# Differential attention: two maps in three adjacent PSUM banks, scores two units ahead, the maps added on GpSimd

## The reference

```
def diff_attention(q, k, v, lam):            # q, k: 4 heads x 2 maps x 64; v: 4 heads x 128
    ...
    def block(qi):                           # blocks of 128 queries
        s = jnp.einsum("bhqtd,bhktd->tbhqk", qi, k).astype(jnp.float32) * scale
        pr = jax.nn.softmax(s, axis=-1)
        a = pr[0] - lam * pr[1]
        return jnp.einsum("bhqk,bhkv->bhqv", a.astype(v.dtype), v)
    ...
o_da = (rmsnorm(o_da, p["da_subln"]) * (1.0 - lam_init))
```

## Time and profile before

| what | value |
|---|---|
| median of three runs | 2616.13 us (2613.88 to 2620.17) |
| time of the profiled execution | 2614.22 us |
| its span, first to last instruction | 2612.5 us |
| PE busy, share of the span | 2406.2 us, 92% |
| DVE busy | 949.7 us, 36% |
| ACT busy | 629.8 us, 24% |
| POOL busy | 403.7 us, 15% |

### The profile page before, as it was taken

One profiled execution on the slowest core, in us unless ns is written; L12 is line 12 of the kernel. 1 busy time (PEld: TensorE's weight loads), 2 busy tenths in 40 slices (PEclk: granted clock), 3 DMA queues, 4 the chain that ended last, 5 costly groups with the idle time before them and its releaser, 6 DMA issues. The chain is left out here.

```text
span 2612.5 us, 36229 instructions
## 1 busy us (share of the span) xinstructions
PE 2406.2 (92%) x13804; PEld 1439.5 (55%) x13804; DVE 949.7 (36%) x1850; ACT 629.8 (24%) x1519; POOL 403.7 (15%) x456
## 2 busy tenths in 40 slices
PE   5999999989999999899779999998999999989995
PEld 2445644466557655555445565545655765555552
DVE  1423411473106423522364143137410642452226
ACT  2223401350015003122132252016001510312221
POOL 0003100021002300133410030000300230013333
PEclk7999999999999999899879999999999999999998
DMA  8443146100544030589653221220022403155985
GB/s 318 160 162 122 65 149 224 43 1 33 169 145 115 33 125 23 200 332 405 241 218 125 86 94 40 84 73 1 33 89 81 129 33 110 39 204 207 377 343 215
DMA packets 170173, 368.55 MB, mean 141 GB/s; under 512 B 38564, under 2 KB 52140, under 8 KB 170036
## 3 DMA queue, kind: packets, MB, share of 16 engines
q1 hardware_dynamic: 121876, 261.49, 27.4%
q10 hardware_dynamic: 24480, 54.76, 6.0%
q0 software_dynamic: 23680, 50.43, 5.9%
HBM read 344.19 MB, written 47.56 MB: 150 GB/s over the span
## 5 line engine op out<-in xcount | busy, mean ns | idle before, releaser
L228 PE MATMUL ps<-hT,ring 128*128 128x512 f32 x512 | 230.9, 605 | 6.3 <-PEq L1147 2.7
L2513 PE MATMUL ps<-ring,mixT 128*32 128x256 f32 x2688 | 214.0, 382 | 2.9 <-DMA ring<-in_w_e_up 2.5
L237 PE MATMUL ps<-ring,hT 128*128 128x512 f32 x480 | 211.9, 598 | 5.1 <-PEq L1191 4.1
L2513 PEld LDWEIGHTS ps<-ring,mixT 128*32 128x32 f32 x2688 | 120.3, 111 | 95.7 <-issue 21.8
L228 PEld LDWEIGHTS ps<-hT,ring 128*128 128x128 f32 x512 | 96.7, 193 | 130.4 <-issue 130.2
L237 PEld LDWEIGHTS ps<-ring,hT 128*128 128x128 f32 x480 | 90.5, 192 | 115.5 <-issue 113.6
L1278 PE MATMUL ps<-late,ring 128*128 128x320 f32 x512 | 147.2, 447 | 7.6 <-PEq L1366 3.9
L2391 PE MATMUL ps<-ring,mixT 128*128 128x512 f32 x320 | 142.1, 603 | 9.2 <-DVE out_xn L2680 4.8
L1278 PEld LDWEIGHTS ps<-late,ring 128*128 128x128 f32 x512 | 99.6, 196 | 52.9 <-issue 14.8
L1229 POOL TENSOR_TENSOR mix_S<-ring 128x512 f32<-128x512 f32 x16 | 25.2, 1577 | 651.1 <-POOLq L1366 550.1
L664 PE MATMUL ps<-hT,ring 128*128 128x512 f32 x256 | 114.5, 601 | 2.9 <-ACT ssm_dec L916 2.9
(11 more groups left out here) (475 smaller groups left out, 4164.1 us busy)
## 6 DMA issues: line engine op xcount, KB each, us to landing
ring<-in_w_in SPq DMA_DIRECT2D x18, 2048.0 KB, 9.8
ring<-in_w_gate SPq DMA_DIRECT2D x12, 2048.0 KB, 10.1
ring<-in_w_e_down SPq DMA_DIRECT2D x48, 512.0 KB, 17.2
ring<-in_w_e_gate SPq DMA_DIRECT2D x40, 512.0 KB, 5.3
ring<-in_w_e_up SPq DMA_DIRECT2D x40, 512.0 KB, 6.6
co_yg<-y_rows SPq DMA_DIRECT2D x40, 512.0 KB, 5.3
mixT<-in_w_ada ACTq DMA_DIRECT2D x8, 2048.0 KB, 8.7
da_ada_w<-in_w_ada ACTq DMA_DIRECT2D x8, 2048.0 KB, 8.8
```

The lines of the kernel that those rows point to most:

```text
L228: pe.matmul(lat, wide[:, k, c], hT[:, k, CTX:TOK], start=(k == 0), stop=(k == kt_n - 1))
L237: last = pe.matmul(out, cx.hT[:, k, tok(t)], wide[:, k, :], start=(k == 0), stop=(k == KT - 1))
L2513: ins = pe.matmul(ps[rows, 2 + b, 0:2 * P].rearrange("p (g f) -> p g f", g=2), xT[:, b, k, rows], ew[:, :, k, :], start=(k == 0), stop=(k ...
```

## The change

It has four parts.

1. **Banks.** The two maps of a unit fill three adjacent banks instead of four: map 0 takes columns 0 to 639 of the three banks' 1536, map 1 the last 640, so that each has one full bank and 128 columns of the middle one. Banks 0 to 2 and 3 to 5 serve in turn. The four products become 512, 128, 512 and 128 columns. The two pieces in the middle bank are kept apart by a new wait of PE, `da_short`, before the last product; and `maxima(u, 1)` waits until the first exponential of its unit has been read, as both touch the middle bank. Maxima and exponentials now read 640 columns in a row.
2. **Two units ahead.** `scores(u+2)` stands where `scores(u+1)` stood, and waits for the second exponential of unit u. `e` gets a third unit (`e_all`, [P, 3, 2, 640]), laid over the rotary tables and lambda, which are done with by then; `sm` gets a third column. ACT's order becomes `exps(u+2, 0)`, `evacuate(u)`, `exps(u+2, 1)`, and DVE's `combine(u)`, `maxima(u+1, 1)`, `maxima(u+2, 0)`, `take(u-1)`.
3. **The maps added on GpSimd.** L1737 goes. DVE ends `combine` with the coefficient; GpSimd then multiplies `e1` by it (128x640) and adds it to `e0` (128x640), and raises `da_a_ready`.
4. `combine(u)` waits also for GpSimd to be done with unit u-2.

```
+            for u in range(len(units)):
+                pool.wait_ge(sem("da_co"), u + 1)
+                e0, e1 = e_all[:, u % 3, 0, :], e_all[:, u % 3, 1, :]
+                pool.tensor_scalar(e1, e1, co[:, u % 2:u % 2 + 1], None, ALU.mult).then_inc(sem("da_scaled"), 1)
+                pool.wait_ge(sem("da_scaled"), u + 1)
+                pool.tensor_tensor(e0, e0, e1, ALU.add).then_inc(sem("da_a_ready"), 1)
...
             def scores(u):
...
-                if u:
-                    pe.wait_ge(sem("da_exp"), 2 * u - 1)
+                if u >= 2:
+                    pe.wait_ge(sem("da_exp"), 2 * u - 2)
...
-                for m in range(2):
-                    pe.matmul(ps[:, b[m], 0:320], q[m], k[m][:, CTX:CTX + 320], start=True, stop=True)
-                for m in range(2):
-                    pe.matmul(ps[:, b[m] + 1, 0:320], q[m], k[m][:, CTX + 320:CTX + 640], start=True,
-                              stop=True).then_inc(sem("da_scores"), 1)
+                short, long = slice(0, KEYS - SEC), slice(KEYS - SEC, KEYS)
+                pe.matmul(to[0][:, 0:SEC], q[0], k[0][:, 0:SEC], start=True, stop=True)
+                pe.matmul(to[1][:, short], q[1], k[1][:, short], start=True, stop=True).then_inc(sem("da_short"), 1)
+                pe.matmul(to[1][:, long], q[1], k[1][:, long], start=True, stop=True).then_inc(sem("da_scores1"), 1)
+                pe.wait_ge(sem("da_short"), u + 1)
+                pe.matmul(to[0][:, SEC:KEYS], q[0], k[0][:, SEC:KEYS], start=True, stop=True).then_inc(
+                    sem("da_scores0"), 1)
...
             def maxima(u, m):
                 n = 2 * u + m
-                dve.wait_ge(sem("da_scores"), n + 1)
-                b = s_banks(n)
-                if n >= 4:
+                dve.wait_ge(sem(f"da_scores{m}"), u + 1)
+                if m:
+                    dve.wait_ge(sem("da_exp"), n)
+                elif n >= 4:
                     dve.wait_ge(sem("da_exp"), n - 3)
...
             def combine(u):
...
                 if u >= 2:
                     dve.wait_ge(sem("da_o_out"), u - 1)
-                step(dve, dve.reciprocal(rc[:, u % 2, :], sm[:, u % 2, :]))
...
-                dve.scalar_tensor_tensor(out=e0, in0=e1, scalar=co[:, u % 2:u % 2 + 1], in1=e0, op0=ALU.mult,
-                                         op1=ALU.add).then_inc(sem("da_a_ready"), 1)
+                    dve.wait_ge(sem("da_a_ready"), u - 1)
+                step(dve, dve.reciprocal(rc[:, u % 2, :], sm[:, u % 3, :]))
+                dve.tensor_scalar(co[:, u % 2:u % 2 + 1], sm[:, u % 3, 0:1], rc[:, u % 2, 1:2], ls[:, 5:6],
+                                  ALU.mult, ALU.mult).then_inc(sem("da_co"), 1)
```

More of the change, by code:

```diff
@@ L1382, in stage_da @@
         nmx = sb("da_nmx", [P, 2, 2])
-        sm = sb("da_sm", [P, 2, 2])
+        sm = sb("da_sm", [P, 3, 2])
         rc = sb("da_rc", [P, 2, 2])
@@ L1425, in _, with score_map @@
             cx.clear_passed(pool)
-        def s_banks(n):
-            return 2 * (n % 3)
+            for u in range(len(units)):
[4 more added lines that the diff above has]
+                pool.tensor_tensor(e0, e0, e1, ALU.add).then_inc(sem("da_a_ready"), 1)
+        KEYS = PAST + LAT
+        def score_map(u, m):
+            unit = ps[:, 3 * (u % 2):3 * (u % 2) + 3, :].rearrange("p b n -> p (b n)")
+            return unit[:, 0:KEYS] if m == 0 else unit[:, 3 * SEC - KEYS:3 * SEC]
         @block.tensor
@@ L1538, in turn @@
                 for c in range(1, 5):
-                    pe.transpose(ps[:, 6, (c - 1) * P:c * P], e[:, u % 2, 0, c * P:(c + 1) * P], cx.ident)
+                    pe.transpose(ps[:, 6, (c - 1) * P:c * P], e_all[:, u % 3, 0, c * P:(c + 1) * P], cx.ident)
                 if u:
                     pe.wait_ge(sem("da_o_out"), u)
-                pe.transpose(ps[:, 7, 0:P], e[:, u % 2, 0, 0:P], cx.ident).then_inc(sem("da_turned"), 1)
+                pe.transpose(ps[:, 7, 0:P], e_all[:, u % 3, 0, 0:P], cx.ident).then_inc(sem("da_turned"), 1)
             def values(u):
@@ L1553, in _ @@
             scores(0)
+            scores(1)
             for u in range(len(units)):
-                if u + 1 < len(units):
-                    scores(u + 1)
+                if u + 2 < len(units):
+                    scores(u + 2)
                 if u:
@@ L1622, in exps @@
                 n = 2 * u + m
-                if u >= 2:
-                    act.wait_ge(sem("da_turned"), u - 1)
+                if u >= 3:
+                    act.wait_ge(sem("da_turned"), u - 2)
+                elif u == 2:
+                    act.wait_ge(sem("da_roped"), 8)
                 else:
@@ L1649, in root @@
                                scale=1.0 / (2 * DA_HD), bias=cx.eps[:, :]).then_inc(sem("da_rms"), 1)
-            exps(0, 0)
-            exps(0, 1)
+            for u in range(2):
+                exps(u, 0)
+                exps(u, 1)
             for u in range(len(units)):
-                if u + 1 < len(units):
-                    exps(u + 1, 0)
-                    exps(u + 1, 1)
-                else:
+                if u + 2 < len(units):
+                    exps(u + 2, 0)
+                elif u + 1 == len(units):
                     root(0, TILES - 1)
                 evacuate(u)
+                if u + 2 < len(units):
+                    exps(u + 2, 1)
                 if u == 2:
@@ L1758, in _ @@
             maxima(0, 1)
+            maxima(1, 0)
             for u in range(len(units)):
@@ L1761, in _ @@
                 if u + 1 < len(units):
-                    maxima(u + 1, 0)
                     maxima(u + 1, 1)
+                if u + 2 < len(units):
+                    maxima(u + 2, 0)
                 if u:
```

26 lines of the change are left out of this document (11 added, 15 removed).

## The result

The changed kernel takes 2632.22 us in the median (2624.69 to 2651.11, 20 runs) against 2617.47 us (2607.46 to 2632.6, 20 runs) for the kernel before on the same chip: ratio 1.0063, 95% interval [1.005, 1.0077]. It is slower by 14.75 us by the medians and by 16 by the ratio (13 to 20 by its interval). Forecast were 2610 us and a range of 2602 to 2621. Its profiled execution took 2629.01 us, with a span of 2627.2. Three executions that lasted 5011 to 7336 us (one each of e4, of e10 and of the kernel before) are in no ratio.

What follows compares the result with a forecast made beforehand. A ring of waits through DVE, 3.92 us per unit, was taken to bound the loop; 66.05 us per layer becoming 63.0 saved 6.1 us in two layers, giving 2610 us, range 2602 to 2621.

Steps and rivals of the forecast that it cites:

- What bounds the loop: Loop before the change: no engine is full, a ring of waits sets the pace at 3.92 us per unit.
- DVE's ring: DVE's cycle before the change: reciprocal, adding the maps, maxima, wait for the second exponential; 3.92 us per unit.
- The new ring: Changed loop: cycle through GpSimd spanning two units, 4.57 us plus scale and add, 7.10 us, 3.55 per unit.
- What GpSimd takes: GpSimd's two steps on 640 columns: scaling 1.0 us (between 0.79 and 1.29), add 1.53 us.
- The bank layout: Score products of 512 and 128 columns: no added cost, at most 0.25 us per unit.
- Rival B: Score products start strictly one behind the other: scores 1.53 us instead of 1.28, 2614 us in all; chance 0.12.
- The start: Unit 0: fifth transpose 8.80 us after the first scores instead of 6.32, 2.5 us lost per layer.
- The clock: Start of the loop: PE's low clock lasts into steady work and costs 1.5 us per layer, bounds 0 and 2.5.
- The end: Last step of the loop: 3.0 us between the last two fifth transposes, as no scores lie between.
- The sum: First scores to last fifth transpose, per layer: 8.80 + 14 x 3.55 + 3.0 + 1.5 = 63.0 us against 66.05.
- C: GpSimd's scaling costs as much as the repeated product, 1.29 us: 3.69 per unit, 2614.7 us in all; chance 0.11.
- D: GpSimd's scale and add, stretched beside DVE work, pace the loop; gain gone at 2.9 us; 2625 us; chance 0.15.

Runs made afterwards that it cites:

- e4: Changed kernel with GpSimd's scaling written as a product of two tensors, the second repeating the coefficient; ratio to the kernel before 1.002 [0.9999, 1.0041].
- e10: Changed kernel with the short score product first, scaling on VectorE, only the adding on GpSimd, ScalarE's squares spread; ratio to the kernel before 0.9943 [0.9923, 0.9962].
- e1: Changed kernel with the maps added on VectorE again instead of GpSimd; ratio to the kernel before 0.9986 [0.9971, 1.0].
- e3: Changed kernel with the maps added on VectorE again and the short score product ahead of the long one; ratio to the kernel before 0.9976 [0.9961, 0.9991].
- e2: Changed kernel with map 1's 128-column score product ahead of map 0's 512-column one; ratio to the kernel before 1.0028 [1.0011, 1.0045].

## Why the prediction was wrong, step by step

- **What bounds the loop: right.** A ring of waits, not an engine; cutting DVE's ring does shorten the unit (e1, e3).
- **The new ring: right in each of its members that had a row.** Take, coefficient, pair, turn, scores, values over two units was given as 4.57 us without the pair. With the measured 1.88 and 1.53 and 0.33 more in the scores that is 8.31; measured 8.30 (single members are off by up to 0.06 both ways). The alternation of a short and a long step came too.
- **What GpSimd takes: the step that failed first.** The add was right (1.53). The scaling was put at 1.0 us, "bounds" 0.79 and 1.29; it is 1.88, outside both. The upper bound was a row of another form on the same engine, and it was taken as a bound because that form reads more. e4 shows the row was right for its own form (1.25) and no bound for this one. The Trainium skill (GPSIMD Engine Reference, § 4, When to use GPSIMD) has one input roughly at line-rate; here it costs more than two inputs do (1.88 against 1.53). Per layer: 14 steps x 0.44 and 0.88 at the start, 7.0 us.
- **The bank layout: the second step that failed.** It was put at 0, bound 0.25, and cost 0.33. The mechanism was not the one given (the pieces in strict order) but the one set aside in a sentence, "the new wait itself ends when 128 columns are through". The columns were through; the signal was behind the long product (e2). Per layer 7 x 0.33 in the ring and 0.34 at the start, 2.7 us.
- **Rival B: its sign came, not its mechanism.** The values began 1.61 us behind the scores, where B had 1.5 to 1.53; but with the short piece first, pieces as unequal run in 1.28 (e2), so they don't line up. By the Trainium skill (TensorE: Matmul & The Clock Gate, Part 3, "What overlaps and what doesn't") products start and end in program order. The starts agree with it: 529.95, 529.96, 530.28 and 530.92 in e2's rows, where only the second passes interleave (the third product starts at 530.28, the second product's second pass at 530.49). For the ends the trace has two answers: the modelled end of the short product's record (494.82) lies ahead of the long one's (495.43), its signal behind, and that was the loss.
- **The start: right in kind.** 8.80 forecast, 10.49 measured; scaling 0.88 and scores 0.34 are most of the difference, and 0.36 more are unit 0's four transposes at the low clock (0.91 where 0.55 was reckoned). **The clock** was put at 1.5 a layer, for 4 us at the low level; it lasted 6.8. The fourteen steps from the first fifth transpose on sum to 59.8 us in layer 0 and 59.2 in layer 1, 1.7 and 1.1 more than 7 x 8.30: the size is right to 0.4.
- **The end:** 3.0 forecast, 3.48 and 4.26 measured. In layer 0 unit 15 waits 0.48 for the add, and the pair was left out of that step; in layer 1 it is the low clock (values 2.49 in place of 1.38) that makes it longer.
- **The sum** corrected: 63.0, scaling 7.0 and wait 2.7 make 72.7, from durations alone. The rest is what the loop itself shows against the forecast's terms, so that it closes by its making: start 0.5, clock 0.2 and end 0.5 in layer 0 (73.9, measured 73.78), start 0.5, clock -0.5 and end 1.3 in layer 1 (74.0, measured 73.92). Two layers of 10.8 more than forecast are 21.7 us, and the median is 22.2 above the 2610 of the forecast.
- **Rivals.** C (a slow scaling) was the right one in kind and had its ceiling too low; C and B together were not priced at all. D named the right condition, slower from a pair of 2.9 us on, and the wrong cause (stretching); the pair is 3.41 us with no stretching. At that length D's own arithmetic gives 7.0 back per layer (0.88 at the start and 14 x 0.44) against 3.05 saved, 4.0 lost, and the wait's 2.7 makes it 6.7 of the 7.7 by which the loop grew. The chance of slower, 0.15, rested on D's cause alone and not on all ways to get over 2.9 us. The row for the stretching was read too simply as well: in the earlier trace rows the add of 1.26 us, taken as the undisturbed one, lies beside the same VectorE step as the one of 2.39.

## What to carry to other kernels

Moving work to an idle engine costs its latency on every ring it joins, however idle the engine is; sum the ring with the price of that very form of operation, and where no row shows the form, a neighbour's price is no upper bound. Turn the sum round and ask from which price on the sign changes: here 2.9 us for the pair, with 1.53 of it known, left 1.4 for a step of unknown form. And here an engine's wait for its own product was released only behind the longer product ahead of it, so put the product that is waited for first.

## What the runs showed of the hardware

- GpSimd, float32, 128x640: a tensor times a number per row 1.88 us, times a constant 1.81, times a tensor that repeats one number 1.25, a sum of two tensors 1.53. The two forms that read one tensor are the slowest. VectorE does the first in 0.55.
- On PE, two products on different halves of the rows run side by side with unequal sizes too (1.28 us for 640 columns on either half, e2), but the wait for a short one that stands behind a long one ended only after the long one: the waiting product started 0.07 us behind the long one's end. Written in the other order it started 0.16 ahead of that end. That signals come in program order is inferred from these two orders.
- PE's granted clock can fall again inside a loop in which PE waits: to 0.50 at the end of layer 1 of the changed kernel, where ten values records took 2.49 us in place of 1.38.
